# The MLP, per-layer embedding and differential projection in one program, with the gate columns projected first

## The reference, cut to what matters

```
m = rms_norm(h, mlp_norm);  h = h + square(relu(m @ w_mlp_up)) @ w_mlp_down
gate = sigmoid(rms_norm(h, ple_norm) @ w_ple_gate + b_ple_gate)
h = h + (p @ w_ple_proj) * gate                                  # x_lat of the second block
h_lat = rms_norm(x_lat, norm_gain) * (1 + sc) + sh               # 1024 tokens x 1024
h_ctx = rms_norm(ctx,   norm_gain) * (1 + sc_c) + sh_c           # 256 context tokens
q, k, v, z = split(h_lat @ da_w_in, 4);  k_c, v_c from h_ctx @ da_w_in
q, k = axial_rope(q), axial_rope(k)                              # latent tokens only
# then differential attention over 1280 keys, a head norm times silu(z), @ w_out, a final norm
```

## Time and profile before

| | us |
|---|---|
| median of three runs | 2510.11 |
| lowest and highest | 2505.64, 2520.14 |
| the profiled execution's own time | 2506.48 |
| its span, first to last instruction | 2504.4 |
| last `project` of the embedding to first differential product | 1489.8 to 1534.7 of the span |
| differential products | 1534.7 to 1933.6 of the span |

### The profile page before, as it was taken

One profiled execution on the slowest core, in us unless ns is written; L12 is line 12 of the kernel. 1 busy time (PEld: TensorE's weight loads), 2 busy tenths in 40 slices (PEclk: granted clock), 3 DMA queues, 4 the chain that ended last, 5 costly groups with the idle time before them and its releaser, 6 DMA issues. The chain is left out here.

```text
span 2504.4 us, 31862 instructions
## 1 busy us (share of the span) xinstructions
PE 2281.3 (91%) x12292; PEld 1887.4 (75%) x12292; DVE 1106.9 (44%) x1920; ACT 980.4 (39%) x1951; POOL 878.2 (35%) x761
## 2 busy tenths in 40 slices
PE   6999476979999999999999986999998799999797
PEld 5799245977888888888887874888887588888455
DVE  4554475861422222222224344443100688888334
ACT  5433453872512112211214334332121577777431
POOL 4423142543323122212312216221110577777432
PEclk9999588999999999999999997999999899999899
DMA  4455645532112012111201103766441635533322
GB/s 144 110 161 136 220 136 158 126 74 69 50 48 68 30 47 59 40 45 51 68 26 43 59 18 99 212 186 192 132 117 56 157 89 125 141 89 93 115 96 84
DMA packets 202279, 248.47 MB, mean 99 GB/s; under 512 B 63592, under 2 KB 123384, under 8 KB 202128
## 3 DMA queue, kind: packets, MB, share of 16 engines
q1 hardware_dynamic: 196368, 240.14, 33.4%
q10 hardware_dynamic: 5760, 6.29, 0.8%
HBM read 172.88 MB, written 65.10 MB: 95 GB/s over the span
## 5 line engine op out<-in xcount | busy, mean ns | idle before, releaser
L1994 POOL TENSOR_TENSOR rm_w_lo<-rm_stage,rm_w_hi 128x512 fp32r<-128x512 f32 x160 | 204.8, 1296 | 552.9 <-ACT rm_w_hi L2021 552.3
L2021 ACT ACTIVATE rm_w_hi<-rm_stage 128x512 fp32r<-128x512 f32 x160 | 97.6, 625 | 286.3 <-PE rm_down L325 233.2
L325 PE MATMUL rm_down<-rm_w_hi,rm_h_hi 128*128 128x512 f32 x512 | 203.3, 397 | 0.0
L2751 DVE TENSOR_REDUCE da_low_score<-da_scores 128x1 f32<-128x1280 f32 x128 | 190.3, 1487 | 29.3 <-PE da_scores L2633 29.2
L325 PE MATMUL rm_down<-rm_w_hi,rm_h_lo 128*128 128x512 f32 x512 | 202.5, 395 | 0.0
L325 PE MATMUL rm_down<-rm_w_lo,rm_h_hi 128*128 128x512 f32 x512 | 202.5, 395 | 0.0
L2734 POOL TENSOR_TENSOR da_prob<-da_prob 128x1280 f32<-128x1280 f32 x64 | 188.1, 2939 | 5.3
L2149 DVE TENSOR_TENSOR residual<-residual,rm_down 128x512 f32<-128x512 f32 x128 | 87.5, 687 | 224.5 <-PE rm_down L325 223.9
L2633 PE MATMUL da_scores<-da_k_hi,da_q 128*128 128x512 f32 (+1 forms) x384 | 151.0, 393 | 34.5 <-DMA da_k_lo<-dk_lo 30.6
L2692 ACT ACTIVATE da_prob<-da_scores,da_low_score 128x1280 f32<-128x1280 f32 x128 | 170.5, 1332 | 7.4 <-DVE da_low_score L2751 7.3
L2140 DVE TENSOR_TENSOR rm_act_r<-rm_act_r 128x512 f32<-128x512 f32 x64 | 45.5, 710 | 222.5 <-ACT rm_act_r L2058 222.5
(11 more groups left out here) (394 smaller groups left out, 6343.2 us busy)
## 6 DMA issues: line engine op xcount, KB each, us to landing
rm_stage<-in_w_mlp_up SPq DMA_DIRECT2D x64, 256.0 KB, 2.8
rm_stage<-in_w_mlp_down SPq DMA_DIRECT2D x64, 256.0 KB, 2.9
dp_stage<-in_da_w_in SPq DMA_DIRECT2D x64, 256.0 KB, 3.3
gla_ada_w<-in_ada_w SPq DMA_DIRECT2D x12, 1024.0 KB, 7.1
da_k_hi<-dk_hi SPq DMA_DIRECT2D x32, 320.0 KB, 9.5
da_k_lo<-dk_lo SPq DMA_DIRECT2D x32, 320.0 KB, 11.1
dp_swapped<-dp_x SPq DMA_DIRECT2D x128, 64.0 KB, 2.1
da_q<-dq SPq DMA_DIRECT2D x32, 256.0 KB, 8.1
```

The lines of the kernel that those rows point to most:

```text
L325: last = nc.tensor.matmul(out, x, y, start=(n == 0), stop=(n == total - 1))
L1994: nc.gpsimd.tensor_tensor(lo, stage[:, n % SLOTS], hi.bitcast(F32), ALU.subtract).then_inc(w_lo_ready, 1)
L2021: nc.scalar.activation(hi, stage[:, n % SLOTS], ACT.Copy).then_inc(w_hi_ready, 1)
L2751: nc.vector.tensor_reduce(out=low_score[:, n, z:z + 1], in_=scores[z][:, 0:K], op=ALU.min, axis=AX.X).then_inc(low_score_ready, 1)
```

## The change

`norm_transpose`, `half_parts` and `differential_project` are gone, and `residual_mlp_ple` becomes `residual_to_differential`, one block with one chain of weight chunks:

- The order of the groups is z, z, q, q, k, k, v, v. The chunks of the first z group are loaded and split during the second half of the embedding's rounds, one per round.
- The third norm goes tile by tile, as the other two do, in the same `scaled` buffer: tiles 0 to 3 are turned behind rounds 9 to 12, tile 4 behind the last round, tiles 5 to 7 behind the results 0, 1 and 2, and the two context tiles behind results 10 and 14. ACT writes 8 high parts of 128x128 (Identity, gain and bias), DVE 8 full values of 128x128 into two buffers of 512, POOL takes two differences of 128x512 (`shifted_low`).
- Results go over 6 banks instead of 8; two are kept for turning. SP asks for each context tile behind the load of a weight chunk (results 3 and 11), and for the rotation's tables behind that of result 8.
- The last stores of the block are those of a v result, high and low part, where they were those of a z result.
- The context's parts and the projection's tiles lie in the memory of the embedding's tiles; the out_lo buffer is `act_r`, the one that also is `scaled`.

```diff
-            residual_mlp_ple(nc, c, a)
-            c.renew_semaphores()
-            with ExitStack() as inner:
-                ...
-                    norm_transpose(nc, c, "n4", half_parts(c, c.mod_gain[:, 0], c.mod_bias[:, 0]) + ...
-                differential_project(nc, c, a, d, ctx_hi, ctx_lo)
+            residual_to_differential(nc, c, a, d)
...
+    GROUPS = (("z", 0), ("z", 1), ("q", 0), ("q", 1), ("k", 0), ("k", 1), ("v", 0), ("v", 1))
+        turn_bank = (down_bank[3:5], up_bank[1:3], up_bank[1:3])
+        dp_bank = (up_bank[0], down_bank[4], down_bank[1], down_bank[0], down_bank[3], down_bank[2])
...                                                              # SP
-            for n in range(PROJ_AT + SLOTS, CHUNKS):
+            for n in range(PROJ_AT + SLOTS, DP_AT + KT + 2):
                 load(n)
+            for n in range(N):
+                p = outs[n][0]
+                m = dp_chunk(p + 1, n - first_of[p] + 2)
+                if n - first_of[p] < KT and m < CHUNKS:
+                    load(m)
+                if n == FT - 1:
+                    load_context(0)
+                if n == KT:
+                    load_table(0)
+                if n == FT + KT - 1:
+                    load_context(1)
...                                                              # POOL
+            def shifted_low(t):
+                for b in range(2):
+                    pool.wait_ge(full_ready, 2 * t + b + 1)
+                    hi, lo = ((ctx_hi, ctx_lo) if t >= TT else (c.Xhi.halves[b], c.Xlo.halves[b]))
+                    ...
+                    nc.gpsimd.tensor_tensor(lo[:, ks, tok], full[b].rearrange("p (k n) -> p k n", n=P),
+                                            hi[:, ks, tok].bitcast(F32), ALU.subtract).then_inc(x_lo_ready[2], 1)
+            for m in range(KT):
+                split_lo(dp_chunk(0, m))
+                if 1 <= m < 6:
+                    token_rstd(2, m - 1)
+                if 2 <= m < 6:
+                    shifted_low(m - 2)
...                                                              # ACT
+            for t in range(TT):
+                sigmoid(TT + t)
+                split(dp_chunk(0, t))
+                if 1 <= t < 6:
+                    modulated_square(t - 1)
+                if 2 <= t < 6:
+                    x_high(2, t - 2)
+            modulated_square(5)
+            x_high(2, 4)
...                                                              # DVE
+            for n in range(GATES):
+                t = n - TT
+                gated(n)
+                if 1 <= t < 6:
+                    scale(2, t - 1)
+                if 2 <= t < 6:
+                    shifted(t - 2)
+            scale(2, 5)
+            shifted(4)
...                                                              # PE
-                    if t:
+                    if t and i == 2:
+                        pe.wait_ge(full_ready, 2 * (t - 1) + b + 1)
+                    elif t:
                         pe.wait_ge(x_lo_ready[i], KT * (t - 1) + 4 * (b + 1))
...
+                if TT < n < TT + 5:
+                    turn(2, n - TT - 1)
+            turn(2, 4)
...
+            pe.wait_ge(x_lo_ready[2], TT)
             for n in range(N):
+                if n == FT:
+                    pe.wait_ge(x_lo_ready[2], 2 * TT)
+                if outs[n][1] == "context":
+                    pe.wait_ge(x_lo_ready[2], 2 * TILES)
+                result(n)
+                if n < 3:
+                    turn(2, 5 + n)
+                for j in range(CT):
+                    if n == KT + 2 + 4 * j:
+                        turn(2, TT + j)
```

More of the change, by code:

```diff
@@ L1989, in _ @@
+            store(N - 1)
+            for i in range(2):
+                sp.wait_ge(stored[i], 16 * sum(1 + has_low[m] for m in range(i, N, 2)))
         @block.gpsimd
@@ L2020, in split @@
                 hi, _ = parts(n)
+                p = (n - DP_AT) // KT
+                if p in (0, 1):
+                    act.wait_ge(gate_ready, TT * (p + 1))
+                elif p >= 2:
+                    act.wait_ge(result_ready, done_at[p - 2])
+                if p >= 0 and sorted_columns(p):
+                    for b in range(2):
+                        last = nc.scalar.activation(pair_member(hi, b, True), pair_member(stage[:, n % SLOTS], b, False),
+                                                    ACT.Copy)
+                    last.then_inc(w_hi_ready, 1)
+                    return
                 nc.scalar.activation(hi, stage[:, n % SLOTS], ACT.Copy).then_inc(w_hi_ready, 1)
@@ L2088, in _ @@
             pt_high(1)
-            for n in range(GATES):
-                act.wait_ge(logit_ready, n + 1)
-                nc.scalar.activation(logit[:, n % 2], logit[:, n % 2], ACT.Sigmoid).then_inc(sig_ready, 1)
+            for n in range(TT):
+                sigmoid(n)
                 if n + 2 < KT:
@@ L2172, in _, with gated @@
             pt_low(1)
-            for n in range(GATES):
+            def gated(n):
                 half, t = divmod(n, TT)
@@ L2184, in _, with shifted @@
                     add_bias(n + 2)
+            def shifted(t):
+                z = t // TT
+                for b in range(2):
+                    dve.wait_ge(x_hi_ready[2], KT * t + 4 * (b + 1))
+                    if t:
+                        dve.wait_ge(x_lo_ready[2], 2 * (t - 1) + b + 1)
+                    for j in range(4):
+                        k = 4 * b + j
+                        last = nc.vector.tensor_scalar(full[b][:, tok_of(j)], turn_bank[2][b][:, tok_of(j)],
+                                                       c.mod_gain[:, z, k:k + 1], c.mod_bias[:, z, k:k + 1],
+                                                       ALU.mult, ALU.add)
+                    last.then_inc(full_ready, 1)
@@ L2186, in _ @@
+            for n in range(N):
+                if n - 1 in rope_index:
+                    low(n - 1)
+                if n in rope_index:
+                    rotate(n)
+                elif has_low[n]:
+                    low(n)
         @block.tensor
@@ new lines, in result @@
+                    ww = w_hi[:, p % 2, k], w_lo[:, p % 2, k]
+                    if kind == "v":
+                        xs = tuple(turned_place(2, at, part, k) for part in range(2))
+                        terms.append((xs, ww))
+                    else:
+                        xs = ((ctx_hi[:, k, :], ctx_lo[:, k, :]) if kind == "context" else
+                              (c.Xhi[:, k, cols_of(at)], c.Xlo[:, k, cols_of(at)]))
+                        terms.append((tuple(y[:, tok_of(f)] for y in ww), xs))
```

566 lines of the change are left out of this document (236 added, 330 removed).

## The result

The changed kernel takes 2477.86 us, the median of four runs (2474.93 to 2479.49), against 2511.10 for the kernel before (four runs, 2505.64 to 2520.14). The ratio is 0.9856 with a 95% interval of 0.9839 to 0.9872, or 33 us less. A second set of runs on another chip gave 2480.26 against 2512.86, ratio 0.9860 (0.9836 to 0.9884). The forecast was 2477.0, in a range of 2465 to 2492.

The account below looks back on a forecast made before the run. PE bounds the kernel, but stands in a chain between embedding and second result. 50.6 - 10.2 - (1.0 + 3.3 + 1.9) - 1.7 - 1.5 = 31.0 us gives 2475.5; half the 3.6 to the median makes 2477, range 2465 to 2492.

Parts of the forecast that it names:

- removed: 56.0 less the first result's own work: From the last `project`'s end to the second result: 56.0 us less 5.4 of work, so 50.6 us of PE can go.
- ten turns: Ten tiles turned between products, 8 transposes each at 1.03 us, all on PE's path: 10.2 us.
- waits in the rounds: Embedding rounds with turns of tiles 0 to 3: DVE's full values just fit; 0.3 us for each of three tiles, 1 us.
- handover, tile 4: Behind turn 3 only three `project`s cover DVE's and POOL's work before result 0: 3.3 us lost.
- turns 5 to 7: Each turn behind one result of 5.45 us, waiting for the tile before's full values: 0.9, 0.5 and 0.5, 1.9 us.
- clock behind the handover: After the handover's waits TensorE's clock falls as after the MLP's norm: 1.7 us, between 0 and 3.4.
- end: Last product to first score: a v result last adds a low part and longer store, 1.5 us, at least 0.7, at most 4.
- All hidden: 128x128 forms as quick as the old ones, waits 1 or 2 us, no clock fall: 37.4 us gained, 2469; chance 0.15.
- The chain is slower: Identity at 0.43 and full values at 0.6 bring waits in rounds, handover and results: 18.5 us gained, 2488; chance 0.16.
- DVE and POOL: They block each other: each round's addition and scaling pay 1.07 us, 10 us less gain, 2487; chance 0.09.
- It doesn't do what it says: Some wait holds the products until the embedding is over; only 5 to 15 us saved, 2495 to 2504; chance 0.05.
- slower, by the clock: PE stops at turns 0 to 7 and the clock stays at 1.2 GHz: 43 us lost, 2520; chance 0.03.

Follow-up runs that it names:

- lead_and_root: Changed kernel with gates' lead cut from three rounds to two from round 9, and POOL's roots of tiles 6 and 7 one weight split earlier: 2478.33 us, ratio 0.9854.

## Why the prediction was right

By its own steps, in PE's path. "Measured" is worked out from the starts of PE's instructions, before and after:

| step | predicted | measured |
|---|---|---|
| removed: 56.0 less the first result's own work | 50.6 | 50.8 |
| ten turns | 10.3 (10 x 1.03; the sum has 10.2) | 9.0 (10 x 0.90) |
| waits in the rounds | 1.0 | 0.2 |
| handover, tile 4 | 3.3 | 3.5 |
| turns 5 to 7 | 1.9 | 1.6 |
| clock behind the handover | 1.7 | 1.2 |
| end | 1.5 (0.7 + 0.7) | 1.3 |
| **gain** | **31.0** | **34.0** (the table: 34.0) |

**What was removed** is 0.2 more by the distance of starts, since the last `project`'s 0.39 overlaps what would follow it.

**The turns** were the term most off. I took the length of the merged row (1.03) for its cost. The distance to the next product is what counts: 0.79, and 0.1 for that one. A round with a turn is 7.72 us (1486.16 to 1493.88 between two turns), against 6.82 without, the 0.90 once more. Ten times 0.13 are 1.3 us.

**The rounds** have no wait: they are 3.8 us longer, four turns (3.6) and 0.2. I had let DVE finish 0.3 us late in three of them. It was in time, since its full values went every 0.32 and not every 0.35 (four in 1.36, the next row starting 1.28 later), and the high parts on ACT came at 0.34 to 0.37 where I had 0.33. Both lay inside their bounds, and neither was near the Copy's 0.25.

**The handover** came as worked out: result 0 starts 8.3 us behind the end of turn 3 (1494.91 to 1503.18), forecast 8.4. In PE's path it is 8.51 us from the product behind turn 3 (1494.67), of which three `project`s are 4.2 and a turn 0.8; the rest is the table's 3.5. I had one wait at the end in mind, released by POOL. PE's rows show it split in three, the larger ones at turn 4 for DVE's full values, and POOL's only 0.40. The chain was right, and the last link small, since the earlier waits lie in front of it on the same engine. They sum to 2.57, where I had 3 to 4. Of the other 0.9, some 0.8 is turn 4 itself, whose halves took 0.63 and 0.95 without the waits instead of 0.8 together, at a granted clock of 0.87.

**Turns 5 to 7** show waits of 0.41, 0.30 and 0.32, and from turn 5 (1509.81) to the product behind turn 7 (1524.98) are 15.2 us, where two results (10.9) and three turns (2.7) need 13.6. The 1.6 are more than the 1.03 of waits, since a turn in two halves pays a little more than one in a piece. The wait at turn 5 has a cause that I hadn't priced there: see the third rival.

**The clock** fell as in rows 9. From result 0 to turn 5 took 6.63 us for 5.45. The price taken from one stall of the MLP's norm, 1.7, was near enough, since a part of it stands in turn 4 above. From the last `project` to the second result are 12.4 us (1498.87 to 1511.23), where I had written about 15.

**Six banks, the context, the tables of ACT** cost nothing, as said. ACT loaded one table, for Silu, at 1507.35 with 1.28 us, in a pause of 2.7 us ahead of result 0's output.

**The rivals.** *All hidden* (2469) fell at the handover and turns 5 to 7, whose waits are there. *The chain is slower* (2488) fell by the sizes of the small instructions. *DVE and POOL* didn't come about where I priced it: the additions in the rounds with turns take 0.69, because POOL has only the small instruction of a root beside them (1481.58 to 1482.13, the addition from 1481.69). The last two, in the handover beside POOL's difference and splits, take 1.27 and 1.06, and the splits grow too:

```profile
1503.08 3.44 POOL L2022 TENSOR_TENSOR rm_w_lo<-rm_stage,rm_w_hi 128x512 fp32r<-128x512 f32 x2
```

Two splits take 3.44 us, 1.74 each, where two alone are 2.6. Behind them POOL makes the root of tile 5, and DVE's scaling of tile 5 waits 2.10 us for it. So this rival did reach the path in the changed kernel, at turn 5, whose wait is 0.41; how much of it is due to those 0.8 us wasn't tested by a run. The run lead_and_root fell into the same thing, with a loss of 1.03 us a tile. The Trainium skill's SBUF — State Buffer (Terms, shared port pair) says that the loser "fully blocks". The scaling of 1503.41 ended at 1505.19; its own 0.75 behind the end of the split (1504.65) would be 1505.40, so the trace agrees to 0.2 us. VectorE's full values, read from PSUM, were not slowed. *It doesn't do what it says* fell with a result 0 that starts 4.3 us behind the last `project`, and *slower, by the clock* with granted clocks of 1.00 in the rounds and 0.80 in one result alone. The rivals' 2469 and 2488 leave out the half way of 1.8 us that the forecast has.

**The total** was right partly by luck. The gain is 3.0 us larger than the sum, and so the changed kernel by the profiled execution should be 2472.5. The profiled execution of before was one that came early to the stretch (1396.7; in the other twelve profiles of this study it was between 1397.2 and 1409.6). I had seen it stand 3.6 under the median and went half the way. Going the whole way, 2510.1, with the measured 34.0 gives 2476.1, and with my 31.0 gives 2479.1. The half way took away 1.8 us of my missing 3. The rule that needs no luck: add the predicted difference to the median, since the time in front of the stretch has nothing to do with the change.

**What stays open.** Why the linear attention stage goes now at the quick and now at the slow level of the clock wasn't tested. Nor was how much of turn 5's wait in the changed kernel comes from VectorE and GpSimd holding each other up.

## What to carry to other kernels

Before you merge two stages, write the ring of one tile (turn, square, root, scaling, full values) with the rows' durations and lay it beside the distance of two tiles in the new order: where the ring is shorter, as with 7.7 us per round here, a stage of 45 us becomes 0.9 us per tile; where only 4 us are left, as at the last tile, it is the ring that you pay. Count a short instruction on a full engine by the distance of starts, not by its length. When VectorE works from SBUF to SBUF on the chain, look at what GpSimd does in that microsecond; a wait on GpSimd can be a gain.

## What was new of the hardware

- A VectorE scaling of 128x1024 from SBUF to SBUF took 1.78 us instead of 0.75 beside one GpSimd tensor_tensor of 128x512; VectorE's 128x128 full values from PSUM took 1.36 for four, beside GpSimd or not. GpSimd's tensor_tensor stayed at 1.30 where it had begun before the scaling, but grew to 1.74 each for two that ran beside VectorE's additions of 128x512 in SBUF (these took 1.27 and 1.06 instead of 0.69).
- A block with the clearing of one semaphore cost 0.4 us or less in the handover.
- Stalls on TensorE cost more than their length here. The handover's stalls of 2.6 us took 1.2 more in the next result; taking them and their followers away, 3.4 us by the list, gave 6.0. With two banks, stalls of 2.66 and 2.43 us were followed by a granted clock of 0.61 and 0.66 over the next result, which took 4.43 and 4.20 us instead of 2.80; behind a stall of 1.18 us, which ended at 1637.68, it stayed at 1.00 and the next result took 5.58 instead of 5.44.
- Eight transposes of 128x128 cost 0.90 us between products at a granted clock of 1.00; four of them took 1.09 where it was 0.56.
- The same stretch of 517 us repeated within 0.2 us between two executions, while the time in front of it lay between 1396.7 and 1409.6 us over thirteen profiles.
